# Layer 1's key/value, query and output weights as plain float32 products in a two-layer trunk kernel

## What is computed

```python
def mla_mixer(h, w_in, q_lora_norm, kv_lora_norm, w_uq, w_ukv, q_norm, k_norm, w_out, cos, sin):
    z = h @ w_in                                     # 1024 -> 256 + 128 + 32
    c_q, c_kv, k_rope = jnp.split(z, (C_Q_RANK, C_Q_RANK + C_KV_RANK), axis=-1)
    c_q = rms_norm(c_q, q_lora_norm)
    c_kv = rms_norm(c_kv, kv_lora_norm)
    q = (c_q @ w_uq).reshape(B, S, C_HEADS, C_QK)    # 256 -> 16 x 96
    kv = (c_kv @ w_ukv).reshape(B, S, C_HEADS, C_NOPE + C_V)   # 128 -> 16 x 128
    ...
    out = dense_chunk_causal_attention(q, k, v, C_QK ** -0.5)
    return out.reshape(B, S, C_OUT) @ w_out          # 1024 -> 1024
...
        x = x + mla_mixer(h, ...)
        h = rms_norm(x, l1_norm_ffn)
        x = x + moe_swiglu(h, l1_router, l1_exp_w_gu, l1_exp_w_down)
```

## Time and profile before

| | |
|---|---|
| median of 3 runs | 1250.08 us (1250.06 to 1251.47) |
| span of the profiled execution | 1247.9 us |
| PE busy | 1208.8 us, 97% |
| DVE busy | 530.3 us, 42% |
| ACT busy | 336.5 us, 27% |
| layer 1's low-rank products and heads | 326 to 352 us |
| layer 1's attention and output products | 352 to 420 us |
| router and first gather | 420 to 432 us |
| experts | 432 to 1243 us |

### The profile page before, as it was taken

How to read it: one execution, slowest core, us unless ns; L and a number is a source line. 1 busy time by engine, 2 the same in 40 slices (tenths; PEclk the granted TensorE clock), 3 DMA queues, 4 the chain that set the end, 5 groups by cost and what they waited for, 6 DMA issues and landing times.

```text
span 1247.9 us, 22143 instructions
## 1 busy us (share of the span) xinstructions
PE 1208.8 (97%) x9410; PEld 594.7 (48%) x9410; DVE 530.3 (42%) x1085; ACT 336.5 (27%) x654; POOL 64.0 (5%) x87
## 2 busy tenths in 40 slices
PE   9988999999988999999999999999999999999987
PEld 7767888888777733333433333333333333333321
DVE  6977665555777411331331143243232141413313
ACT  7365555454766300110220011011010012001101
POOL 5300000000530000000000000000000000000000
PEclk9999999999999999999999999999999999999999
DMA  9503545454605999999999999999999999999995
GB/s 345 196 19 138 195 176 187 182 196 121 231 6 223 385 383 418 397 380 417 423 420 423 423 421 422 423 422 406 423 423 421 423 422 421 423 423 420 422 423 233
DMA packets 61001, 413.58 MB, mean 331 GB/s; under 512 B 7120, under 2 KB 7280, under 8 KB 12640
## 3 DMA queue, kind: packets, MB, share of 16 engines
q1 hardware_dynamic: 60048, 411.20, 81.2%
q0 software_dynamic: 560, 0.81, 0.5%
q10 hardware_dynamic: 288, 0.08, 0.0%
HBM read 411.02 MB, written 1.05 MB: 330 GB/s over the span
## 4 chain that ended last, share of the span: by engine, by line
PE 82%; DVE 5%; SPq 4%; DMA 3%; ACT 3%; issue 1%; POOL 1%; DVEq 0%; ACTq 0%; POOLq 0%
PE PS L2465 37%; PE PS L2475 18%; PE PS L1936 6%; PE PS L1938 6%; PE PS L1937 6%; SPq L586 4%; DMA homes<-in_expert_tiles 2%; PE PS L2342 2%; DMA ring<-in_dense_tiles 1%; DVE w_lo L1243 1%; PE PS L2004 1%; PE PS L2049 1%; ACT arena L839 1%; PE PS L2374 1%; PE PS L1957 1%
## 5 line engine op out<-in xcount | busy, mean ns | idle before, releaser
L2465 PE MATMUL PS<-homes,arena 128*32 128x512 f32 x3736 | 409.7, 592 | 3.3 <-DMA homes<-in_expert_tiles 3.3
L2465 PEld LDWEIGHTS PS<-homes,arena 128*32 128x32 f32 x3736 | 120.1, 110 | 282.4 <-issue 270.5
L2475 PE MATMUL PS<-homes,arena 128*32 128x512 f32 x1928 | 213.5, 593 | 4.4 <-DMA homes<-in_expert_tiles 4.4
L1823 DVE SCALAR_TENSOR_TENSOR arena<-arena,PS 64x256 f32<-64x256 f32 x126 | 52.2, 414 | 379.2 <-ACT arena L1179 377.2
L1179 ACT ACTIVATE arena<-PS 64x512 f32<-64x512 f32 x63 | 37.3, 592 | 462.7 <-PE PS L2465 462.7
L1936 PE MATMUL PS<-w_hi,hT_hi 128*128 128x512 f32 (+2 forms) x372 | 141.8, 381 | 5.1 <-DVE w_lo L1243 3.0
L1938 PE MATMUL PS<-w_hi,hT_lo 128*128 128x512 f32 (+2 forms) x372 | 139.3, 374 | 0.0
L1937 PE MATMUL PS<-w_lo,hT_hi 128*128 128x512 f32 (+2 forms) x372 | 139.2, 374 | 0.0
L2475 PEld LDWEIGHTS PS<-homes,arena 128*32 128x32 f32 x1928 | 61.5, 110 | 149.8 <-issue 138.0
L2465 PE MATMUL PS<-arena 128*32 128x512 f32 x928 | 103.2, 592 | 2.2 <-DVE arena L1830 1.7
L1243 DVE TENSOR_TENSOR w_lo<-ring,w_hi 128x1024 fp32r<-128x1024 f32 (+1 forms) x60 | 66.9, 1160 | 32.8 <-ACT w_hi L784 32.6
(11 more groups left out here) (241 smaller groups left out, 1008.3 us busy)
## 6 DMA issues: line engine op xcount, KB each, us to landing
homes<-in_expert_tiles SPq DMA_DIRECT2D x270, 1024.0 KB, 20.2
arena<-in_expert_tiles SPq DMA_DIRECT2D x54, 1024.0 KB, 22.0
ring<-in_dense_tiles SPq DMA_DIRECT2D x49, 1024.0 KB, 4.8
arena<-in_expert_tiles SPq DMA_DIRECT2D x8, 512.0 KB, 7.3
arena<-in_expert_tiles SPq DMA_DIRECT2D x16, 256.0 KB, 7.5
x_res<-in_expert_tiles SPq DMA_DIRECT2D x4, 1024.0 KB, 10.3
ring<-in_dense_tiles SPq DMA_DIRECT2D x6, 512.0 KB, 6.2
ring<-in_dense_tiles SPq DMA_DIRECT2D x2, 832.0 KB, 4.3
```

Source lines behind the costliest of these rows:

```text
L1823: ins = v.scalar_tensor_tensor(out=act_exp[64 * j:64 * (j + 1), g, :], in0=gate[0:64, g, c], scalar=1.0, in1=PS[0:64, gu_banks[k][g], c], ...
L2465: ins = pe.matmul(PS[GROUP * q:GROUP * (q + 1), gu_banks[k][g], :], xT[:, cc, o + g * GROUP:o + (g + 1) * GROUP], quarter(k_home, q), star ...
L2475: ins = pe.matmul(PS[GROUP * q:GROUP * (q + 1), 3 + g, :], tokens_T(k, c, q // 2, g), quarter(k_home, q), start=k == 0 and c == 0, stop=end)
```

## The change

The pieces from `UKV` on (index `NSPLIT`, 51) are no longer split. PE reads them from the ring and multiplies each block and chunk with one plain float32 matmul. The activations for these products are one float32 copy: `lT` for the low-rank columns, written by ACT with the norm weights as scale (three instructions of 128 columns for a tile of tokens), and `mT` for the merged heads, three halves copied by DVE and the last by ACT. A ring place of such a piece is free when PE has used the piece and no longer when it is split. Since `w_hi`, `w_lo` and `hT_lo` have their last use earlier, `HOME_OF` lists their places first: 14, the six split places, two of the ring, 13, then the two early ones, the three late ones, the other four of the ring, 12, and `x_res`.

```diff
+NSPLIT = STREAM.index(UKV[0])
...
-HOME_OF = [14] + [(U0 - RING + i) % RING for i in range(RING_FIRST)]
+HOME_OF = [14]
+for _i in range(SLOTS):
+    HOME_OF += [RING + (NSPLIT - SLOTS + _i) % SLOTS, RING + SLOTS + (NSPLIT - SLOTS + _i) % SLOTS]
+HOME_OF += [(U0 - RING + i) % RING for i in range(RING_FIRST)]
+HOME_OF.append(13)
+
+EARLY_HOME = SLAB_HOMES + LATE_HOMES
+HOME_OF += range(EARLY_HOME, EARLY_HOME + len(EARLY))
 HOME_OF += range(SLAB_HOMES, SLAB_HOMES + LATE_HOMES)
 HOME_OF += [(U0 - RING + i) % RING for i in range(RING_FIRST, RING)]
...
+HOME_OF.append(12)
...
+        mT = placed("mT", [P, KC, SEQ], f32, 12)
+        lT = placed("lT", [P, 3, SEQ], f32, 13)
...
-                if u >= RING:
+                if RING <= u < NSPLIT + RING:
                     sp.wait_ge(lo_ready, 2 * (u - RING + 1))
+                elif u >= RING:
+                    sp.wait_ge(used, u - RING + 1)
...
+                elif k < RING and last_in_ring(k) < NSPLIT:
+                    sp.wait_ge(lo_ready, 2 * (last_in_ring(k) + 1))
                 elif k < RING:
-                    sp.wait_ge(lo_ready, 2 * (U0 - (U0 - 1 - k) % RING))
+                    sp.wait_ge(used, last_in_ring(k) + 1)
                 elif k < RING + 2 * SLOTS:
-                    sp.wait_ge(used, U0 - (U0 - 1 - (k - RING)) % SLOTS)
+                    sp.wait_ge(used, NSPLIT - (NSPLIT - 1 - (k - RING)) % SLOTS)
+                elif k == 13:
+                    sp.wait_ge(used, first(OUT1))
...
-                if v < U0:
+                if v < NSPLIT:
                     split_piece(v, piece_floats(STREAM[v]))
...
-                split_half(i0 + 2, 1, 0, 4)
-                split_half(i0 + 3, 1, 1, 5)
+                if kind == "AB":
+                    split_half(i0 + 2, 1, 0, 4)
+                    split_half(i0 + 3, 1, 1, 5)
+                else:
+                    split_bank(i0 + 3, mT[:, 4:8, P:2 * P], bank(5).rearrange("p (c n) -> p c n", c=4))
...
-                split_bank(X_LORA + t, hT_hi[:, 0:3, t * P:(t + 1) * P],
-                           bank(6 + t)[:, 0:3 * P].rearrange("p (c n) -> p c n", c=3))
+                a.wait_ge(transposed, X_LORA + t + 1)
+                for c in range(3):
+                    g = 4 * KC + c
+                    ins = a.activation(lT[:, c, t * P:(t + 1) * P], bank(6 + t)[:, c * P:(c + 1) * P], ACT.Copy,
+                                       scale=gains[:, g:g + 1])
+                ins.then_inc(hi_split, 1)
...
+            def merged_half(i, t, g, b):
+
+                v.wait_ge(transposed, i + 1)
+                v.tensor_copy(mT[:, 4 * g:4 * g + 4, t * P:(t + 1) * P], bank(b).rearrange("p (c n) -> p c n", c=4))\
+                    .then_inc(lo_split, 1)
...
                 c0, w = STREAM[u][2], STREAM[u][4]
+                if u >= NSPLIT:
+                    pe.wait_ge(ring_loaded[u % RING], 16 * (u // RING + 1))
+                    for c in range(k0, k1):
+                        o = (c - c0) * w
+                        ins = pe.matmul(out, mT[:, c, t * P:(t + 1) * P], ring[:, u % RING, o:o + w],
+                                        start=c == 0, stop=c == KC - 1)
+                    return ins
...
-                    piece_wait(u, o)
-                    ins = product(bank(4 * t + n), hT_hi[:, 2, t * P:(t + 1) * P], hT_lo[:, 2, t * P:(t + 1) * P],
-                                  w_hi[:, u % SLOTS, o:o + COLS], w_lo[:, u % SLOTS, o:o + COLS], True, True)
+                    ins = pe.matmul(bank(4 * t + n), lT[:, 2, t * P:(t + 1) * P], ring[:, u % RING, o:o + COLS],
+                                    start=True, stop=True)
```

More of the change, by code:

```diff
@@ L592, in _, with last_in_ring @@
                 load(u, A["dense_tiles"][u, :, 0:n], n)
+            def last_in_ring(k):
+                return U0 - 1 - (U0 - 1 - k) % RING
             def first_free(m):
@@ L872, in attention @@
                         split_ahead(ahead[HI_AHEAD.index(j)])
-                    if j == 4:
+                    if j == 4 and kind == "AB":
                         split_half(i0, 0, 0, 5)
-                    if j == 5:
+                    if j == 5 and kind == "AB":
                         split_half(i0 + 1, 0, 1, 1)
-                split_half(i0 + 2, 1, 0, 4)
-                split_half(i0 + 3, 1, 1, 5)
+                if kind == "AB":
[3 more added lines that the diff above has]
+                    split_bank(i0 + 3, mT[:, 4:8, P:2 * P], bank(5).rearrange("p (c n) -> p c n", c=4))
             a.dma_start(ident[:, :], A["ident"]).then_inc(ident_loaded, 16)
@@ L1083, in _ @@
             attention(16, "C", [first(UQ) + i for i in range(len(UQ))], X_MERGE1)
-            for i in range(len(OUT1) - 2):
-                after(first(OUT1) + i)
             for g in range(2):
@@ L1254, in split_ahead @@
                 w = u + SLOTS
-                if w < U0:
+                if w < NSPLIT:
                     split_piece(w, piece_floats(STREAM[w]))
@@ L1305, in query_scale @@
                 link(v.tensor_scalar(q_scale[:, 1, t, c0:c0 + nh], s, -scale, None, ALU.mult))
+            def merged_half(i, t, g, b):
+                v.wait_ge(transposed, i + 1)
+                v.tensor_copy(mT[:, 4 * g:4 * g + 4, t * P:(t + 1) * P], bank(b).rearrange("p (c n) -> p c n", c=4))\
+                    .then_inc(lo_split, 1)
             def attention(s0, kind, ahead, i0):
+                half_done = split_half if kind == "AB" else merged_half
                 def front(i):
@@ L1399, in attention @@
                     if j == 5:
-                        split_half(i0, 0, 0, 5)
+                        half_done(i0, 0, 0, 5)
                     if j == 6:
-                        split_half(i0 + 1, 0, 1, 1)
+                        half_done(i0 + 1, 0, 1, 1)
                     if j in LO_AHEAD:
@@ L1408, in attention @@
                         final(j // 4, 1)
-                split_half(i0 + 2, 1, 0, 4)
-                split_half(i0 + 3, 1, 1, 5)
+                half_done(i0 + 2, 1, 0, 4)
+                if kind == "AB":
+                    split_half(i0 + 3, 1, 1, 5)
                 split_ahead(ahead[2])
@@ L1591, in _ @@
             for t in range(NT):
-                s = (slice(None), slice(0, 3), slice(t * P, (t + 1) * P))
-                split_bank(X_LORA + t, hT_lo[s], hT_hi[s], bank(6 + t)[:, 0:3 * P].rearrange("p (c n) -> p c n", c=3))
                 o = R_OFF[R_LORA + t]
@@ L1986, in attention @@
                 m0, u0 = s0 // 4, first(pieces)
+                l0 = i0 if kind == "AB" else i0 - NT
                 def scores(i):
@@ L2031, in values @@
                     if i == 12:
-                        pe.wait_ge(lo_split, i0 + 1)
+                        pe.wait_ge(lo_split, l0 + 1)
                     maps = 1 if kind == "AB" and p < 4 else 2
@@ L2086, in attention @@
                 chunk_products(u0, 0, bank(0), 2, 4)
-                pe.wait_ge(lo_split, i0 + 2)
+                pe.wait_ge(lo_split, l0 + 2)
                 chunk_products(u0 + 1, 0, bank(0), 4, 8).then_inc(early_out, 1)
@@ L2135, in rest_of_out @@
                 u0 = first(pieces)
+                l0 = i0 if pieces is OUT0 else i0 - NT
                 for i in range(2):
-                    pe.wait_ge(lo_split, i0 + 3 + i)
+                    if pieces is OUT1 and i == 1:
+                        pe.wait_ge(hi_split, i0 + 1)
+                    else:
+                        pe.wait_ge(lo_split, l0 + 3 + i)
                     piece_products(u0 + i, 1, bank(6)).then_inc(used, 1)
@@ L2233, in _ @@
             for t in range(NT):
[L2234 to L2237, removed]
+                pe.wait_ge(hi_split, X_LORA + t + 1)
+                pe.wait_ge(ring_loaded[u % RING], 16 * (u // RING + 1))
                 for n in range(4):
@@ L2251, in _ @@
                     u = first(UQ) + n
+                    pe.wait_ge(ring_loaded[u % RING], 16 * (u // RING + 1))
                     for c in range(C_QR // P):
                         o = c * COLS
[L2254 to L2257, removed]
+                        ins = pe.matmul(bank(4 * t + n), lT[:, c, t * P:(t + 1) * P], ring[:, u % RING, o:o + COLS],
+                                        start=c == 0, stop=c == C_QR // P - 1)
                     if t:
```

## The result

| | before | after |
|---|---|---|
| median of the runs | 1250.24 (4 runs, 1250.06 to 1251.47) | 1255.4 (4 runs, 1252.99 to 1256.76) |
| profiled execution | span 1247.9 | 1252.99, span 1251.2 |
| first expert product | 432.45 | 436.20 |
| last expert tile landed, last 16 matmuls start | 1235.99 | 1239.23 |

The ratio is 1.0041, with a 95% interval of 1.003 to 1.0053: slower by 0.4%, a small change but clear of the noise. The changed kernel run again, with more runs, gave a median of 1253.77 and a ratio of 1.0031 [1.0021, 1.004] (first experiment). The forecast was 1254.0, 3.9 above before; the first four runs stand 5.2 above before, the nine later ones 4.0 above the runs of before beside them (1249.75).

What follows compares the result with a forecast made beforehand. DMA paces the expert part, but with tile places full the end follows the experts' start. Terms +0.4 - 1.9 + 5.4 = +3.9 on 1250.08 gave 1254.0 us; range 1251.8 to 1256.4, reaching down to 1250.6.

Steps and rivals of the forecast that it cites:

- What bounds the kernel: Expert part: DMA paces it but all 21 places fill near 550 and 855, so the end moves as the experts' start.
- the prefetch part: Beside attention: ten expert tiles fetched from about 342 instead of mostly after 386; costed at nothing, ends 0 and 7.7 gain.
- Rival A: Expert part: the lead in fetched tiles counts and removes late waits, -7.7, giving 1246.3; chance 0.08.
- D: Prefetch: it does not come forward because an earlier wait holds the queue; time stays the forecast's; no chance given.
- the 3.4 of the working: Second expert: VectorE marks slots 3.4 us later, hidden by 6.19 us of idle time; without that cover 0 to 1.
- Layer 1, before attention: Low-rank, key/value and query stage: dearer plain products against missing splits; +0.4 us, ends -0.5 and +1.2.
- the clock dip: Granted clock 0.50 at 352 to 354, forecast to stay; if gone, the fill behind ends up to 0.9 earlier.
- rival B: Stages before the experts give 2.5 more back (-0.9 clock, -0.9 first stage, -0.7 attention): 1251.5; chance 0.16.
- In attention: Layer 1's attention, from the fifth head group: copies no longer wait behind splits, two output products dearer; gain of 1.9 us.
- Output products: Output stage, bound by PE alone: 30 plain products each 0.18 dearer than split ones; +5.4 us.
- Rival C: Output stage: the full-height float32 weight load is not hidden, 11 to 14 us more, about 1265; chance 0.04.
- the spreads listed ahead of it: First stage -0.9 to +0.8, attention 1 either way, 0.5 for 30 products' price, 0 to 1 for marking or DMA.

Runs made afterwards that it cites:

- first experiment: The changed kernel run again, unaltered, with more runs; median 1253.77 us of 9 runs, ratio 1.0031.
- the two runs on the lead: Changed kernel with second and later expert tiles waiting for attention's last scores, 1254.2 us; kernel before with nine unused matmuls ahead of the gather, 1253.48 us.
- tiles held back: Changed kernel, but the second and all later expert tiles wait for attention's last scores; median 1254.2 us of 9 runs, ratio 1.0031.
- experts put off: Kernel before with nine more unused float32 matmuls of 256 columns on PE just before the first gather; median 1253.48 us, ratio 1.003.
- splits earlier: Kernel before, all products still split, but the first output pieces' splits moved out of attention's tight spots on ACT and VectorE; median 1247.8 us, ratio 0.9979.
- output part only: Changed kernel, but key/value and query weights and low-rank activations split as before; plain output weights and early prefetch stay; median 1253.38 us, ratio 1.002.
- ACT's copies back: Changed kernel with ACT's three copies of output pieces put back in attention, unused, and most expert tiles waiting for attention's values; 1256.11 us, single execution.
- VectorE's subtractions back: Changed kernel with VectorE's two double subtractions put back in attention, unused, and SP waiting on the last merge; 1260.06 us, single execution.

## Why the prediction held, step by step

**What bounds the kernel, and the prefetch part.** Right. It rested on reading the dips of DMA's share as places run full, and so on the rule that the end follows the start of the experts. The start moved by 3.75, the last tile by 3.24, and the two runs on the lead show the rule both ways. Rival A is refuted. The tiles come from 343.43, not about 342, which cost nothing; D did not come about. The first dip lies at 538 to 542 in before, so the places are full near 540 rather than 550. VectorE's idle time behind the marking in the second expert went from 6.19 to 2.76 in the changed kernel, the 3.4 of the working, and remained a cover:
```profile
612.08 0.68 DVE L1897 TENSOR_TENSOR arena<-arena,PS 64x512 f32<-64x512 f32 x1 [2.76 <-ACT arena L1211]
```
The Trainium skill, "Trainium Kernel Development and Optimization", Best Practices, has double buffering overlap DMA with compute; the trace agrees that the transfers overlap, and the runs show that fetching still earlier is worth nothing once the buffers, here 21 places, are what runs out.

**Layer 1, before attention: +0.4 was too little.** From the low-rank transposes to the second tile's heads' transposes it is 33.61 after (33.60 in its second profile, 33.58 with the tiles held back) and 33.14 before. But this 33.14 holds the clock dip of the earlier trace rows. The kernels with the split low-rank part whose profile has no dip there show 32.87 (experts put off), 32.90 (splits earlier) and 32.92 (output part only). So the part costs 0.7, and the dip cost 0.25. This is the term of the sum that was sized worst. Where the 0.3 went is seen once 0.16 is taken off, by which the whole stage began late (325.69 against 325.53). ACT's timeline of before and of the changed kernel:
```profile
340.47 1.86 ACT L1043 ACTIVATE h_tok<-PS,stat 128x512 f32<-128x512 f32 x3
```
```profile
333.57 1.57 ACT L1044 ACTIVATE arena<-PS,stat 128x256 f32<-128x256 f32 x4 [1.25 <-POOL stat L702]
...
341.35 1.84 ACT L1064 ACTIVATE h_tok<-PS,stat 128x512 f32<-128x512 f32 x3 [0.99 <-PE PS L2288]
```
The copies of the keys start at 333.57, as forecast (333.4 and the 0.16). The query copies start at 341.35, less the 0.16 at 341.19 and not at 341.0: PE took up their products 0.08 later than forecast (335.89), and from there to the copies it was 5.46, where I had put 5.35 (5.15 and 0.2). The remaining 0.1 is in what I compared with: 340.59 stands in the chain, but the copies of before start at 340.47.
I expected the dip to stay and it went; the -0.9 that rival B gave for it was too much, since PE then waits 1.16 at 359.30 for VectorE's copy of the transposed heads.
The Trainium skill, "TensorE: Matmul & The Clock Gate", Part 4, says that transposes don't count for the clock as other work does. By that rule the dip behind the transposes should have stayed. It is in before's profile and in that of the run with ACT's copies (0.50 at 353 to 356), and absent in the other seven though the same transposes and the same pause (1.95 or 1.96) stand there. The runs don't bear the rule out as a forecast for a single execution.

**In attention: -1.9 came out as -2.1.** The mechanism is shown by three runs (the splits earlier, ACT's copies back, VectorE's subtractions back): the 1.4 of the fifth group (from a wait of 1.63 to one of 0.25) is ACT's split, the late merge is VectorE's. PE went on at 381.54 (381.0 forecast, plus the 0.6 by which the stage began late), and at 390.14 (389.7). The six products start at 397.23 (396.8).

**Output products: +5.4 came out as +5.2.** From the six products on to the end of the products it was 21.41 and is 26.63. The term is 0.2 short because the split products cost 0.687 each over the whole stage and not 0.68: the first step behind a transpose takes 0.31 and not 0.23 (414.58 to 414.89). The price of 0.86 for 512 columns, taken from the earlier trace rows at another shape of matmul, holds at full height: 0.43 for each instruction. Rival C, the exposed weight load, is refuted: its sign was a step above 0.5.

**The sum.** +0.7 - 2.1 + 5.2 = 3.8, against +3.9. At the experts' start 3.75 was measured; 0.16 of it stood before layer 1's low-rank transposes, and the dip of before's profile takes 0.25 off. All three terms were off, by +0.3, -0.2 and -0.2, and nearly cancelled: each has the right cause, but that the sum came within 0.1 is in part luck. Rival B had its condition half met (dip gone, attention 0.2 better) and had the first stage the wrong way. The range does not follow from the spreads listed ahead of it: added up they give 1251.6 to 1257.3, and no working leads to 1256.4 or to 1250.6. The median of 1255.4 stands 1.6 above that of the nine later runs; this is no part of the sum, but scatter, in which stretches of low clock have a part. I had taken before's scatter (1250.06 to 1251.47) for the scatter of both, where before itself reaches 1253.29 in 27 runs.

Open: why the granted clock falls in one execution and not in the next, what starts the stretches in layer 0, and what made the expert part and the writing of the output longer in the second profile. The change is no visible cause: nine of its runs lie within 4.9 us of each other, 27 of before within 4.8.

## What to carry to other kernels

When a stage is paced by DMA with a fixed number of places, look first for moments with all places full, as dips of DMA's share while PE is busy: behind the last one only PE's own start counts, and fetching earlier buys nothing. A split of a weight into two parts that takes three cheap products costs other engines time, but if those have room, as here, the order of their work gives all of that back, while a dearer product on the bounding engine stays: before trading engines' work, move the work that stands ahead of a copy PE waits for.

## What the runs showed of the hardware

- A plain float32 product of 128x128 by 512 columns costs 0.86 us (two instructions of 0.43) in a long row, three split steps 0.68. The full-height weight load adds nothing to the plain product: an instruction costs 0.43 with it, and four side by side on 32 columns of the array took 0.429 too.
- Saturated DMA (share 1.01, 424 GB/s) beside attention did not slow it: PE's busy time is 15.93 against 15.95 without it, the scores 1.89 in both.
- The granted clock falls to 0.50, the 1.2 GHz level, in single stretches that change from run to run of one and the same code: at 76 to 79 us in the second profile of the changed kernel and not in the first, at 352 to 355 in before, at 384 to 387 behind a wait of 1.63 in the run with ACT's copies, while before and the kernel with the experts put off have the same wait (1.63 and 1.62) and full clock behind it. In the records of the nine runs of the changed kernel mean clocks of 1.000 and 0.996 go with 1252.1 and 1256.1 us, as much as the whole effect of the change.
The Trainium skill, "TensorE: Matmul & The Clock Gate", Part 1, calls the gate run-variable, for the matmuls at a kernel's start. No run here was read at its start; deep inside the kernel the profiles agree, and vary from execution to execution.
